# Key norms in the attention block, RWKV operand stage in two pair groups, rooted step last

## The reference, cut to what matters

```python
w_log = -softplus(-(b_w0 + tanh(wl) @ b_w2)) - 0.5
decay = exp(-exp(w_log))
a = sigmoid(b_a0 + al @ b_a2)
g = sigmoid(gl) @ b_g2
kk = heads(k * b_kk)
kk = kk * rsqrt(sum(kk * kk, axis=-1) + 1e-12)      # the key norms
k = k * (1.0 + (a - 1.0) * b_ka)
# per token: state = state*w + (state @ -kk) (kk*a)^T + v k^T;  y = state @ r
y = layernorm(y, b_ln_g, b_ln_b)                    # needs a root
out = (y + sum(r * k * b_rk) * v) * g
```

## Time and profile before

| | |
|---|---|
| median of 3 runs | 3648.35 us (3647.73 to 3648.91) |
| profiled execution, its own time | 3652.75 us |
| its span | 3650.9 us |
| PE, DVE, ACT, POOL busy, share of the span | 81%, 71%, 36%, 39% |
| attention window, 208.5 to 272.0 | 63.5 us |
| operand block, 272.0 to 329.0 | 57.0 us |
| recurrence block, 329.0 to 523.3 | 194.3 us |
| tail | 3127.6 us |

### The profile page before, as it was taken

How to read it: one execution, slowest core, us unless ns; L and a number is a source line. 1 busy time by engine, 2 the same in 40 slices (tenths; PEclk the granted TensorE clock), 3 DMA queues, 4 the chain that set the end, 5 groups by cost and what they waited for, 6 DMA issues and landing times.

```text
span 3650.9 us, 38148 instructions
## 1 busy us (share of the span) xinstructions
PE 2975.2 (81%) x11532; PEld 1418.9 (39%) x11532; DVE 2607.3 (71%) x6403; ACT 1328.6 (36%) x3991; POOL 1407.4 (39%) x1223
## 2 busy tenths in 40 slices
PE   7997877887777777999797878988988867777777
PEld 5774763333223223434344333333434313232222
DVE  2675648876766667798978576999777676667664
ACT  3354213333333333336653232345623323333332
POOL 1200004544434434444345354543444434444443
PEclk9997989999999999999899999998999999999999
DMA  4101039999999999999899999998999999999998
GB/s 133 39 15 47 3 93 417 417 415 421 418 421 415 410 422 402 419 409 375 332 416 396 392 421 419 416 418 335 416 421 421 396 422 421 421 418 410 421 420 350
DMA packets 216573, 1293.40 MB, mean 354 GB/s; under 512 B 23600, under 2 KB 41008, under 8 KB 68784
## 3 DMA queue, kind: packets, MB, share of 16 engines
q0 software_dynamic: 165888, 1208.03, 80.6%
q1 hardware_dynamic: 50480, 82.93, 6.5%
HBM read 1286.49 MB, written 3.87 MB: 353 GB/s over the span
## 4 chain that ended last, share of the span: by engine, by line
DMA 43%; PE 21%; DVE 11%; issue 7%; ACT 3%; POOL 1%; DVEq 0%; ACTq 0%; SPq 0%; POOLq 0%
DMA ring<-in_uv,route 41%; PE banks L1577 16%; DVE ring L1517 4%; DVE X L1527 2%; PE banks L1965 1%; ACT route L1562 1%; PE banks L1905 1%; DVE own L2213 1%; ACT route L1547 1%; POOL ring L1506 1%; PE banks L1931 1%; ACT route L1552 1%; PE banks L2374 0%; DMA own<-in_l_peer_wq 0%; DMA own<-in_l_w_in 0%
## 5 line engine op out<-in xcount | busy, mean ns | idle before, releaser
L1577 PE MATMUL banks<-ring,route 128*128 128x512 f32 (+1 forms) x4088 | 1981.7, 621 | 557.9 <-ACT route L1562 549.0
L1506 POOL DMA_INDIRECT ring<-in_uv,route x1152 | 1320.4, 1146 | 1705.3 <-PE banks L1577 1507.0
L1517 DVE SCALAR_TENSOR_TENSOR ring<-ring,XN 128x1024 f32<-128x1024 f32 x1152 | 1408.8, 1223 | 728.6 <-DMA ring<-in_uv,route 725.9
L1577 PEld LDWEIGHTS banks<-ring,route 128*128 128x128 f32 (+1 forms) x4088 | 724.3, 188 | 1648.7 <-issue 823.3
L1547 ACT ACTIVATE route<-route 128x2 f32<-128x2 f32 x576 | 117.3, 204 | 1855.5 <-DVE ring L1517 1855.2
L1562 ACT ACTIVATE route<-IDN,route 128x128 f32<-128x128 f32 x894 | 309.2, 387 | 3.5 <-PE banks L1577 2.3
L1552 ACT ACTIVATE route<-route 128x1 f32<-128x1 f32 x1152 | 276.7, 287 | 23.5 <-ACT route L1547 0.4
L1905 PE MATMUL banks<-own,QP 128*128 128x512 f32 (+1 forms) x400 | 177.7, 567 | 7.8 <-DMA own<-in_l_w_in 5.4
L1527 DVE SCALAR_TENSOR_TENSOR X<-ring,route,X 128x1024 f32<-128x1024 f32 x130 | 166.5, 1281 | 0.9
L1547 ACT ACT_TABLE_LOAD x106 | 136.0, 1283 | 1.9
L1905 PEld LDWEIGHTS banks<-own,QP 128*128 128x128 f32 x400 | 76.7, 193 | 98.0 <-issue 84.2
(11 more groups left out here) (448 smaller groups left out, 3097.6 us busy)
## 6 DMA issues: line engine op xcount, KB each, us to landing
ring<-in_uv,route POOLq DMA_INDIRECT x1152, 13.1
own<-in_l_w_in SPq DMA_DIRECT2D x16, 1024.0 KB, 16.7
own<-in_l_w_out SPq DMA_DIRECT2D x12, 1024.0 KB, 16.5
own<-in_l_peer_wq SPq DMA_DIRECT2D x12, 1024.0 KB, 16.3
X<-in_x_prompt SPq DMA_DIRECT2D x8, 512.0 KB, 8.4
ring<-in_l_w_in SPq DMA_DIRECT2D x4, 1024.0 KB, 9.8
ring<-in_l_peer_wq SPq DMA_DIRECT2D x2, 2048.0 KB, 12.0
own<-in_l_w_in SPq DMA_DIRECT2D x4, 656.0 KB, 15.5
```

Source lines behind the costliest of these rows:

```text
L1506: pool.indirect_dma_start(self.ring[:, s % RING, :], None, self.io[f"uv{of_slot(s)[0]}"], bass.IndirectOffsetOnAxis(ap=self.EI[:, g % 2, k ...
L1517: dve.scalar_tensor_tensor(u, u, 1.0, self.XN[:, of_slot(s)[1], :], ALU.mult, ALU.mult, accum_out=self.HD[:, g % 2, k:k + 1]).then_inc(sel ...
L1577: m = pe.matmul(self.bank[1 + half][0:n, :], self.DG[:, (V_TENSOR[s] - 1) % 4, 0:n], self.ring[:, s % RING, D + 512 * half:D + 512 * half ...
```

## The change

1. A class `KeyNorms` makes the squares, the turned marks SELT, the sums and their root inside the attention block: squares on ScalarE in units 3, 6, 9 and 12, transposes on TensorE in unit 6, the sums in units 18 (512 columns) and 26 (64 columns), the copies in 15, 21 and 29, the root when the 40 units are done. Each piece stands ahead of `turn(u)` on TensorE and between `expo(u+1)` and `copy(u)` on ScalarE.
2. In the operand block T0 and T3 have a buffer for each pair. ScalarE works in groups: gates of pairs 0 and 1, keys and rates of both, exponentials of both, then gates of 2 and 3, then pair 2 and pair 3.
3. The rate product T3 = KN * T3 goes to GpSimd; VectorE waits for it ahead of BB. `scan(1)` moves ahead, `scan(p+2)` behind BB and KB.
4. On VectorE, step 16 of the recurrence comes last in its turn.

```diff
                         for u in range(N):
                             if u + 2 < N:
                                 scores(u + 2)
+                            norms.pe(pe, u)
                             turn(u)
...
                             if u + 1 < N:
                                 expo(u + 1)
+                            norms.act(act, u)
                             copy(u)
+                        norms.act(act, N)
...
+class KeyNorms:
+    def pe(self, pe, u):
+        if u == 6:
+            for p in range(4):
+                m = pe.transpose(self.bank[0:8, p * P:(p + 1) * P], self.SEL[:, 8 * p:8 * p + 8], self.ident)
+            m.then_inc(self.marks.h, 1)
+        elif u in (18, 26):
+            first, n = (0, 512) if u == 18 else (512, TOK - 512)
+            if u == 18:
+                pe.wait_ge(self.marks_out.h, self.marks_out.at(1))
+                pe.wait_ge(self.squared.h, self.squared.at(4))
+            else:
+                pe.wait_ge(self.norms.h, self.norms.at(1))
+            for p in range(4):
+                m = pe.matmul(self.bank[0:8, 0:n], self.SEL[:, 8 * p:8 * p + 8], self.KK[p][:, first:first + n],
+                              start=(p == 0), stop=(p == 3))
+            m.then_inc(self.sums.h, 1)
+    def act(self, act, u):
+        if u in (3, 6, 9, 12):
+            p = u // 3 - 1
+            act.activation(self.KK[p], self.K[p], ACT.Square,
+                           scale=self.BV[:, V_KK + p:V_KK + p + 1]).then_inc(self.squared.h, 1)
+        elif u == 15:
+            act.wait_ge(self.marks.h, self.marks.at(1))
+            act.activation(self.SELT, self.bank[0:8, :], ACT.Copy).then_inc(self.marks_out.h, 1)
+        elif u == 21:
+            act.wait_ge(self.sums.h, self.sums.at(1))
+            act.activation(self.RIN[:, 0:512], self.bank[0:8, :], ACT.Copy).then_inc(self.norms.h, 1)
+        elif u == 29:
+            act.wait_ge(self.sums.h, self.sums.at(2))
+            act.activation(self.RIN[:, 512:], self.bank[0:8, 0:TOK - 512], ACT.Copy).then_inc(self.norms.h, 1)
+        elif u == AH * NT:
+            act.wait_ge(self.norms.h, self.norms.at(2))
+            act.activation(self.RIN, self.RIN, ACT.Sqrt, bias=self.eps).then_inc(self.norms.h, 1)
...
+        spare = Room(wide[:, big.at + 256:])
-        T0S, T3S = (XV[:, 6, 0:TOK], T0N), (XV[:, 7, 0:TOK], T3N[:, :])
+        T0S, T3S = ([spare.take(TOK) for _ in range(4)] for _ in range(2))
...
+                pool.wait_ge(mh.h, mh.at(8))
+                for p in range(4):
+                    pool.wait_ge(kt.h, kt.at(2 * p + 2))
+                    pool.wait_ge(kn.h, kn.at(2 * p + 2))
+                    if p:
+                        pool.wait_ge(tk.h, tk.at(p))
+                    pool.tensor_tensor(T3S[p], KNS[p % 2], T3S[p], ALU.mult).then_inc(tk.h, 1)
...
-                dve.wait_ge(rt.h, rt.at(1))
                 dve.reciprocal(RIN, RIN).then_inc(ri.h, 1)
                 scan(0)
...
+                    if p == 0:
+                        scan(1)
...
-                    ch.add(dve.tensor_tensor(K, K, T2, ALU.mult))
-                    ch(dve.tensor_tensor(T3, KN, T3, ALU.mult))
+                    ch(dve.tensor_tensor(K, K, T2, ALU.mult))
...
-                    if p < 3:
-                        scan(p + 1)
+                    dve.wait_ge(tk.h, tk.at(p + 1))
                     blocks(BB[:, :, p, :], chunks(T3), chunks(T5))
                     blocks(KB[:, :, p, :], chunks(K), chunks(T5))
+                    if p < 2:
+                        scan(p + 2)
...
+                act.activation(LG, LG, ACT.Sigmoid).then_inc(tn.h, 1)
+                for p in range(2):
+                    lora_out(p)
+                for p in range(2):
+                    keys_in(p)
+                    rates(p)
+                for p in range(2):
+                    decays(p)
+                for p in range(2):
+                    last_decay(p)
+                for p in range(2, 4):
+                    lora_out(p)
+                take_v(0)
+                for p in range(2, 4):
+                    keys_in(p)
+                    rates(p)
+                    decays(p)
+                    last_decay(p)
+                    take_v(p - 1)
...
+                lora(0)
+                pe.wait_ge(ri.h, ri.at(1))
+                spread_norms(0)
+                lora(1)
+                turn_v(0)
+                lora(2)
                 for p in range(3):
                     bonus(p)
                     spread_norms(p + 1)
-                    if p + 2 < 4:
-                        lora(p + 2)
-                    turn_v(p)
+                    if p == 0:
+                        lora(3)
+                    else:
+                        turn_v(p)
...
-                for tau, c, k in turns:
+                for tau, c, k in sorted(turns, key=lambda turn: (turn[0], turn[2] == 16)):
```

More of the change, by code:

```diff
@@ L172, in encoder, with attention @@
         stored = sig("stored")
-        def attention(tag, rows, QT, key_of, V_of, SEL, scale, OUT, prefetch, zero):
+        def attention(tag, rows, QT, key_of, V_of, SEL, scale, OUT, prefetch, zero, norms):
             with ExitStack() as st:
@@ L319, in encoder @@
         zl, ll = sig("lora_zeroed"), sig("lora_loaded")
+        norms = KeyNorms(sb, sig, lw, bank, X, PB, BV, MIX, IDN)
         def prefetch(sp):
@@ L332, in encoder @@
                   MSK, float(AQK) ** -0.5, OC,
-                  prefetch, zero)
-        rwkv(nc, io, sb, sig, bank, CST, BV, MIX, PC, lw, W2A, G2, IDN, wide, side, PA, PB, OC, OBT, X)
+                  prefetch, zero, norms)
+        norms.end()
+        rwkv(nc, io, sb, sig, bank, CST, BV, MIX, PC, lw, W2A, G2, IDN, wide, side, PA, PB, OC, OBT, X, norms)
         l0.close()
@@ L756, with __init__, end @@
 V_W0, V_A0, V_KK, V_KA, V_RK, V_LG, V_LB, V_MU = 0, 4, 8, 12, 16, 20, 24, 28
-def rwkv(nc, io, sb, sig, bank, CST, BV, MIX, PC, lw, W2A, G2, IDN, wide, side, PA, PB, OC, OBT, X):
+KEY_FIRST = 4
+class KeyNorms:
+    def __init__(self, sb, sig, stack, bank, X, PB, BV, MIX, IDN):
+        self.bank, self.ident, self.eps = bank[7], IDN[:, 0:128], IDN[0:8, 129:130]
+        self.RIN, self.SELT = (sb(stack, n, [8, w])[:, :] for n, w in (("RIN", TOK), ("SELT", 512)))
+        self.SEL, self.BV = MIX[:, BT + 4:], BV
+        rows = X[:, :, :].rearrange("p t d -> p (t d)").rearrange("p (s n) -> p s n", s=8)
+        self.K = [PB[:, KEY_FIRST + p, :] for p in range(4)]
+        self.KK = [rows[:, 4 + p, 0:TOK] for p in range(4)]
+        self.squared, self.marks, self.marks_out, self.sums, self.norms = (sig(n) for n in (
+            "kk_squared", "marks_turned", "marks_copied", "kk_sums", "kk_norms"))
+    def pe(self, pe, u):
[31 more added lines that the diff above has]
+            act.activation(self.RIN, self.RIN, ACT.Sqrt, bias=self.eps).then_inc(self.norms.h, 1)
+    def end(self):
+        self.squared.end(4), self.marks.end(1), self.marks_out.end(1), self.sums.end(2), self.norms.end(3)
@@ L768, in rwkv @@
+def rwkv(nc, io, sb, sig, bank, CST, BV, MIX, PC, lw, W2A, G2, IDN, wide, side, PA, PB, OC, OBT, X, norms):
     ident, eps = IDN[:, 0:128], IDN[:, 129:130]
@@ L788, in rwkv @@
         B8 = here.take(4, 64)
-        oka, SEL = MIX[:, BT:BT + 4], MIX[:, BT + 4:]
-        T3N, KNS, T1B, T2B = (sb(s2, n, [P, w]) for n, w in (("T3N", TOK), ("KN", 2 * TOK), ("T1B", TOK), ("T2B", TOK)))
+        oka = MIX[:, BT:BT + 4]
+        KNS, T1B, T2B = (sb(s2, n, [P, w]) for n, w in (("KN", 2 * TOK), ("T1B", TOK), ("T2B", TOK)))
         T4B, T5B = sb(s2, "T4B", [P, NCH * (CHK + 1)]), sb(s2, "T5B", [P, TOK])
-        RI, SE = sb(s2, "RIN", [8, TOK]), sb(s2, "SELT", [8, 512])
-        RIN, SELT = RI[:, :], SE[:, :]
+        RIN, SELT = norms.RIN, norms.SELT
+        spare = Room(wide[:, big.at + 256:])
         T4S = more.take(NCH, CHK + 1), T4B[:, :].rearrange("p (c n) -> p c n", c=NCH)
-        T5S, T0N = (more.take(TOK), T5B[:, :]), more.take(TOK)
+        T5S = (more.take(TOK), T5B[:, :])
         T1S, T2S = (XV[:, 4, 0:TOK], T1B[:, :]), (XV[:, 5, 0:TOK], T2B[:, :])
-        T0S, T3S = (XV[:, 6, 0:TOK], T0N), (XV[:, 7, 0:TOK], T3N[:, :])
+        T0S, T3S = ([spare.take(TOK) for _ in range(4)] for _ in range(2))
         KNS = KNS[:, 0:TOK], KNS[:, TOK:]
-        KK2 = KNS + T2S
         chunks = lambda x: x.rearrange("p (c n) -> p c n", c=NCH)
@@ L882, in _, with lora_out @@
             def _(act):
[L883 removed]
+                def lora_out(p):
                     act.wait_ge(za.h, za.at(p + 1))
[L886 to L888 removed]
+                    for i, (dst, col) in enumerate(((T0S[p], V_W0), (T3S[p], V_A0))):
                         act.activation(dst[:, 0:512], bank[i][:, :], ACT.Sigmoid, bias=BV[:, col + p:col + p + 1])
@@ L891, in lora_out @@
                                        bias=BV[:, col + p:col + p + 1]).then_inc(zg.h, 1)
-                    if gate:
-                        gate_out(p)
+                    gate_out(p)
```

62 lines of the change are left out of this document (13 added, 49 removed).

## The result

Twenty executions of the changed kernel have a median of 3654.72 us (3647.50 to 3662.30), twenty of the kernel before, taken beside them, 3647.64 (3643.81 to 3649.80). The medians are 7.1 us apart. The ratio is 1.0018, 95% interval 1.0012 to 1.0024: **slower by 6.6 us, between 4.4 and 8.8**. The forecast was 3647.9 and no change; the time lies 2.5 us above the top of its range. The profiled execution took 3655.53 us, with a span of 3653.8.

A forecast was written before the change was run, and what follows sets the result against it. Attention's TensorE is nearly full, the operand stage is a relay between engines, and the tail follows the recurrence's end. +4.35 - 6.0 + 1.2 = -0.45 on the median 3648.35 gave 3647.9 us, no change; range 3641.8 to 3652.2.

The forecast's parts named there:

- What bounds the kernel: Whole kernel: a shift of the recurrence block's end moves the kernel's end equally; the two edited stages are 120 us, 3.3%.
- Attention, +4.35: Attention block: added sums cost 2.75 us, squares 1.1, the table load and root at the end 0.5.
- Rival (b): Attention takes in the norms, only the root's 0.45 us stays: total -4.35, 3644.0 us; chance 0.08.
- Operand stage, -6.0: Operand stage: walked in the new order, it ends at 51.0 us instead of 57.0.
- the 7.4 us are not gained: Operand stage start: the reciprocal's wait goes, but pair 1's products replace it; first scaled key at 14.3 us, exponentials at 19.0.
- the low bound: Operand stage: gain of only 2.0 us if each of three later TensorE sections stays at the low clock.
- rival (d): Operand stage: GpSimd's product blocks VectorE, four times up to 2.22 us, 8.9; total +8.4, 3656.8 us; chance 0.06.
- Rival (c): Operand stage: TensorE keeps the full clock, -10 us instead of -6, about 3642 us in total; chance 0.08.
- Recurrence, +1.2: Recurrence: seven chunks give 0; in chunk 7 the rooted product stands behind a waiting addition, 1.2 us later.
- Rival (a): Recurrence: reordering hides the root's wait, -5.6 us instead of +1.2; total -7.25, 3641.1 us; chance 0.08.
- The sign given for this: Recurrence: the scalings would still start 0.2 us behind the turned blocks, with one chunk 1.2 us longer.
- three signs of being wrong: Attention growing by under 2 us, the operand stage under 47 us, or a shorter recurrence would refute the forecast.

The follow-up runs named there:

- pool_only: Kernel before with only the key norms moved to attention, their sums one to a unit, plus the rate product on GpSimd: 3646.94 us, ratio 0.9998.
- after_again: The changed kernel run again unaltered, with a second profile: 3654.70 us, ratio 1.0019.
- before_again: The kernel before, unaltered, in a second profiled execution: 3644.21 us.
- order_only: Kernel before with only step 16 of the recurrence put last in its turn on VectorE: 3649.52 us, ratio 1.0006.
- rate_dve: Changed kernel with the rate product back on VectorE: 3648.95 us, ratio 1.0006.
- spread_first: Kernel before with only the norms moved, sums one to a unit, and the next pair's norm spread ahead of the bonus product on TensorE: 3642.79 us.
- best_old: spread_first with pair 0's gate copy also put ahead of its keys on ScalarE: 3637.81 us, ratio 0.9972.
- best_new: Changed kernel with old recurrence order, rate product on VectorE, norm sums one to a unit, and norm spread ahead of the bonus product: 3642.83 us.

## Why the prediction was wrong

**What bounds the kernel**: right. The net of the head went through to the end; nothing behind it took it up.

**Attention, +4.35**: measured 4.9 in the executions at the same clock. The mechanisms and units were right; the sizes were low. The squares cost 0.65 and 0.63, not 0.5 and 0.6; the sums 3.04, not 2.75, since they took 3.53 and not 3.4, and of the pause and the tail set against them (0.65) only about 0.5 was there; the root cost 0.5, as forecast. Rival (b), that attention takes the norms in, is out.

**Operand stage, -6.0**: the step that failed. Measured -2.65 in the first profile and -3.4 in the better executions. Up to bonus(0) the walk held within 0.3 us, and the two landmarks on which "the 7.4 us are not gained" rests came at 14.0 and 18.8. It then had TensorE's last low-rank products at three times 1.12; they ran at 2.08, 2.02 and 1.38 and made pair 3's norm product 2.0 late. The walk had named the low bound, products that stay at the low clock, for the range, and had taken the full clock for the sum. The row that it had, the gap of 3.71 us, has 4.3 us at 0.51 behind it; the products at 308.88 to 313.20 of the same trace, in the same place behind a bonus product and a spread, took 2.08, 2.02 and 1.43, and would have given the 2.0. In the changed kernel the low stretch reached from 298.82 into the product at 307.15, over 8 us of work. The other 1.2 is pair 3's key product beside GpSimd. That step had costed the move to GpSimd at nothing (2.22 hidden behind 3 to 7 us); GpSimd's own time was hidden, 1.4 to 2.3, but what it does to VectorE was not. This is rival (d)'s mechanism, one instruction of VectorE held for 1.2 us in pairs 1 and 3, a size of 1.2 that reaches the path and not 8.9. The Trainium skill, "SBUF — State Buffer", Who interferes with whom, agrees in kind: the two exclude each other for an instruction. pool_only shows it to be no loss by itself, because the work that leaves VectorE is worth as much. So rival (d) names a part of the miss, not the cause of the stage's. The walk also has a slip: 43.7 and 6.9 are 50.6, not 51.0. From pair 3's norm product to the end it took 8.7, and 7.5 without the stretched product, so the 7.3 that its 51.0 implies are about right. Rival (c), the clock stays up, is out: the stage's clock fell from 0.78 to 0.72.

The table loads: the sum went by 1.28 a load and no drain. In the changed kernel the load at attention's end begins at 274.70 and the root at 276.00, the same distance as in the earlier trace rows; the Trainium skill's 1.38 more, "ScalarE: Activation LUTs", What ACT_TABLE_LOAD costs, shows in no gap here either.

**Recurrence, +1.2**: the mechanism measured 1.23, at the chunk forecast. But the recurrence as a whole is +2.4 to +3.2 longer. The remainder comes with TensorE's clock. In all five executions of the changed kernel one step, in chunk 3, takes 19.65 us, at a granted clock of 0.91 in the first profile and in after_again; in before_again it takes 17.68 at 1.00. VectorE hands over the variance for the first root after 43.7 us in the first profile, with a clock of 0.50 over the recurrence's first 20 us, and after 40.7 in after_again, with 0.74 (the kernel before: 42.9 at 0.53, 41.8 at 0.60). A low stretch costs by what it falls on: the kernel before's first profile has one in that step too, at 0.90, and takes 17.89. The forecast carried the clock only inside the stage, as a rival that could only help ((c), clock up). It had no term for where the low stretch would come to lie in the next block. Rival (a) is out: seven chunks gave nothing. The sign given for this, scalings 0.2 behind the turned blocks, did not come: they wait 0.87 in the other chunks as well (order_only, at 372.85), because VectorE is done with its turn sooner, and lose nothing by it.

**The range** failed with it: its upper end took the stage's low bound alone and nothing for the blocks around it. Between the executions at their best the sum is +3.9 in place of -0.45, which from 3648.35 is already the top of the range, 3652.2; the placing of the low stretches does the rest. None of the three signs of being wrong came (attention under 2, stage under 47, recurrence shorter): all three watched for a kernel that is faster.

What stays open is why the low stretches fall where they do. rate_dve has a median 5.7 us under the changed kernel with a head as long as that kernel's best and no execution over 3653.3, so without the GpSimd product the worse placing is not met; in the old order of pairs the same product does nothing (pool_only). No run shows the link between the two. A step of 19.6 to 19.7 in chunk 3 also came with pool_only, spread_first and best_old, so it doesn't belong to the pair groups, as best_new's expectation had it; best_new itself had 18.17 there.

## What to carry to other kernels

When a stage is a relay between engines, look for the small instruction behind which the next engine's input or buffer waits, and move that before regrouping the loop: an earlier gate copy of 0.6 us and one swap of two matmuls took 8.6 us off the stage, while the regrouping with its own buffers made it 2 us longer and won nothing in the median. Before pricing a product at the full clock behind an idle time of TensorE, look for the same run of products in the trace at hand and take its durations; here it was there and was not read. Expect the low stretch to move into the neighbouring block. Work taken from VectorE to GpSimd is worth its length less what VectorE's two-input instructions lose beside it, here about all of it. Test two moves together as well as each alone: here each was level and both together had the long executions.

## What was not expected of the hardware

- A GpSimd product of 128x576 took 1.40 us where it began ahead of VectorE's instruction or alone, and 1.91 to 2.28 where VectorE's began first; a two-input instruction of VectorE that met it took up to 1.97 instead of 0.75.
- In all nineteen profiles every idle time of TensorE of 2.17 us or more within the operand stage was followed by work at 1.2 GHz, 2.07 or 2.08 for a product that takes 1.08 to 1.13 at the full clock; behind one of 2.10 (best_old, at 304.14) it took 1.13.
- The changed kernel's twenty executions differ by up to 14.8 us at a mean granted clock of 0.955 to 0.963, and in the profiled ones the difference lies in few places: stretches at 1.2 GHz that begin some microseconds earlier or later against the code. The lower mean clocks go with the longer times (correlation -0.72).
- A pause of TensorE of 0.45 us that repeats in attention took in about 0.4 of an added sum of 0.88, and no more: single sums, put one to a unit, still cost about 0.5 each.
